# A two-block transformer kernel on one core: packed modulation products, alternating projection blocks, products crossed behind norms and turns in groups

## The chip, the cores and the metric

The kernel runs on one core of a Trainium2 chip. TensorE (PE) multiplies, VectorE (DVE) and ScalarE (ACT) do the element-wise work and empty PSUM, and SyncE (SP) issues the transfers. The metric is the time of one execution on the device in microseconds (us), the median of the runs; less is better.

## The reference

256 tokens of width 1024 go through a first block of two layers (modulated norms, attention, SwiGLU) and a second block of two layers (mLSTM and retention side by side, then a feed-forward part and a gate). Everything is float32.

```python
def first_block(x, c, ctx, c_ctx, ...):                # DEPTH = 2
    for l in range(DEPTH):
        sh_a, sc_a, g_a, sh_f, sc_f, g_f = [m[:, None, :] for m in adaln(c, mod_w[l], mod_b[l])]   # silu(cond) @ mod_w + mod_b
        csh_a, csc_a, cg_a, csh_f, csc_f, cg_f = adaln(c_ctx, mod_w[l], mod_b[l])
        hx = modulate(rms_norm(x, norm_mix_g[l]), sh_a, sc_a)
        hc = modulate(rms_norm(ctx, norm_mix_g[l]), csh_a, csc_a)
        y_x, y_c = even_mixer(...) if l % 2 == 0 else odd_mixer(...)
        x = x + g_a * (y_x @ w_out[l])
        x = x + g_f * swiglu(modulate(rms_norm(x, norm_ffn_g[l]), sh_f, sc_f), ffn_w_in[l], ffn_w_out[l])
        ...                                            # the same for ctx in layer 0
    return x

def second_block(x, p, ...):
    for i in range(DEPTH):
        z = rmsnorm(x, norm1_g[i]) @ w_in[i] + b_in[i]
        _, _, mv, mo, mi, mf, rq, rk, rv, rg, gm, gr = split_cols(z)
        qk = jax.nn.silu(causal_conv(z[..., :2 * M_QK], conv_w[i], conv_b[i]))
        ...
        hm = mlstm_chunkwise(mq, mk, mv, mi, log_sigmoid(mf))
        y_m = sigmoid(mo) * head_layernorm(hm, m_norm_g[i], M_HEADS)
        hr = retention_chunkwise(rope(rq), rope(rk) * R_DK ** -0.5, rv, log_gamma)
        y_r = silu(rg) * head_layernorm(hr, r_norm_g[i], R_HEADS)
        merged = sigmoid(gm) * (y_m @ w_bm[i]) + sigmoid(gr) * (y_r @ w_br[i])
        x = x + merged @ w_out[i]
        x = x + square(relu(rmsnorm(x, norm2_g[i]) @ w_ff1[i] + b_ff1[i])) @ w_ff2[i] + b_ff2[i]
        x = x + sigmoid(rmsnorm(x, norm3_g[i]) @ w_pe_gate[i]) * (p[i] @ w_pe[i])
    return rmsnorm(x, final_g)
```

## The kernel before

**Weights.** All weights come from one array in HBM, cut into 348 chunks of 1 MB: four tiles of 128 rows of the contraction by 512 columns. SP loads them in order into a ring of four slots (`RING`). Most products are made of three: ACT rounds a chunk into `w_hi` (L1085, three slots, `HI_RING`), DVE writes what is left, `w_lo`, in place of the chunk (L1503), the activations are likewise split into `x_hi` and `x_lo`, and `product` (L471 to L476) multiplies hi by hi, lo by hi and hi by lo. 300 chunks go this way; the 48 of the modulation are multiplied as they are. A contraction of 1024 takes two chunks (`kg` 0 and 1) for a block of 512 columns.

**Forms.** `project_feat` gives a block with features on the partitions (256 tokens wide), and its four sub-blocks lie in two banks of PSUM. `project_tok` gives one with tokens on the partitions, 512 wide, in two banks. `project_feat` and `project_tok` alternate between banks 0, 1 and 2, 3 from block to block. `claim(bank)` waits until the bank's last reader is done.

**Order.** The order is written out by hand for each engine. PE's program sets the order of the chunks. ACT and DVE convert chunks at set places of their own programs: `split_for(st, l, j)` (ACT) and `lo_for` (DVE) convert up to `AHEAD` = 2 chunks past the last chunk of a block; `split_to` and `lo_to` go to a given chunk.

**Modulation.** Its 24 blocks of 512 columns are spread over the first block's work. `mod_chunk` (L745) multiplies one raw chunk with the padded condition vectors `cond` (8 matmuls per block at L759), ACT copies the bank to rows (L1240), and `mod_turn` (L731) turns the rows of the block with four small matmuls (L742, two records each in the trace) into columns in bank 4. DVE adds the bias (L1740) and sets `mods_ready` (L1748) for a part of the blocks (`MOD_PARTS`). The first part, blocks 0 to 3, is wanted before the first weight product, that of `ev_in`; squares of X are added for its norm (L584, L587).

**Second block.** Per layer, in PE's order: four blocks mqk (features), the gates, mv and mo (two token blocks each), rqk, then values and scores of the four mLSTM heads (L885, L891) between the blocks rv, those of retention (L903) between gm and gr, turns (`turn`, L599, matmuls at L608) of y_m (`ym`, 8 blocks), w_bm, turns of y_r (`yr`, 16), w_br (8 chunks), turns of merged (`mg`, 8), w_out2 (4 chunks), ff1 and ff2 in halves, pe. For each mqk block DVE scales the result by 1/rms (L1998) into `SCR`, ACT adds the bias and makes the first tap of the convolution (L1410), DVE adds three taps for four channels (12 instructions, L2036) and ACT applies silu. The token blocks get their bias on DVE (L1958, `biased`). `layer_norms` (L1963) norms y_m and y_r on DVE (L1972: subtract the mean, multiply by 1/std, for each head and tile). Behind w_out2 `update` adds to X (L2161), and the tails square X, make `x_hi` (ACT) and `x_lo` (DVE, L1587) as the input of ff1; `after_first` puts the norm's sum of squares after the first chunk of the product behind it.

## Time and profile before

| | |
|---|---|
| median of 3 runs | 2538.41 us |
| lowest, highest | 2537.29, 2539.85 us |
| the profiled execution | 2536.93 us |
| its span on the core | 2535.1 us |
| busy PE / DVE / ACT | 2358.1 / 1520.0 / 1017.4 us |
| mean share of TensorE's full clock | 0.971 |
| moved by DMA | 389.2 MB |

The profile is of one execution. Its views list each engine's instructions with their start, their length and the idle time before them, with what ended that idle time. An idle stretch of an engine that isn't the last to finish costs nothing.

### The profile page before, as it was taken

Reading aid. Unit: us, or ns where it says so; the run is one execution under the profiler, and the core shown is the slowest. Engines: PE = TensorE matmul, PEld = TensorE weight load, DVE = VectorE, ACT = ScalarE, POOL = GpSimd, SP = SyncE. Lnnn points to the kernel's source line nnn. Section 1 sums busy time; section 2 is a strip of 40 time slices with the busy share of each in tenths; the row PEclk is TensorE's granted clock in tenths of the full one; section 3 lists DMA queues with packets and bytes.
Section 4 is the critical chain, followed back from the end, with each engine's and each line's share of the span. In section 5 each row is a group of like instructions: output and inputs, shape, how many; then the busy total and the mean of one; then the engine's idle time right before and its main releaser. Section 6 shows DMA issues by size and latency. Waiting matters only on the chain.

```text
span 2535.1 us, 33331 instructions
## 1 busy us (share of the span) xinstructions
PE 2358.1 (93%) x14334; PEld 2029.4 (80%) x14334; DVE 1520.0 (60%) x1872; ACT 1017.4 (40%) x1222; POOL 0.2 (0%) x4
## 2 busy tenths in 40 slices
PE   5988989999998988999899998999988999999997
PEld 3765667777776757999888876899987978679997
DVE  3787542323246586555666767576666766767575
ACT  4245542221124155334553334444555424344344
POOL 0000000000000000000000000000000000000000
PEclk9989989999998999999999999999999999999998
DMA  6450034444332142555454543455544535344552
GB/s 275 166 199 1 23 138 189 169 163 183 116 106 105 72 100 82 184 183 184 166 195 163 183 170 133 167 177 184 181 153 178 179 145 202 131 161 167 183 183 100
DMA packets 61114, 389.20 MB, mean 154 GB/s; under 512 B 6568, under 2 KB 11048, under 8 KB 15784
## 3 DMA queue, kind: packets, MB, share of 16 engines
q1 hardware_dynamic: 60968, 387.08, 42.2%
q8 instruction: 113, 1.85, 0.3%
q14 instruction: 33, 0.27, 0.0%
HBM read 386.00 MB, written 1.05 MB: 153 GB/s over the span
## 4 chain that ended last, share of the span: by engine, by line
PE 75%; DVE 16%; ACT 5%; issue 3%; DMA 1%; SPq 0%; DVEq 0%; ACTq 0%
PE PS L474 22%; PE PS L475 22%; PE PS L476 22%; DVE w_lo L1503 4%; PE PS L759 2%; DVE BIG L2036 2%; ACT w_hi L1085 1%; PE PS L608 1%; PE PS L903 1%; PE PS L647 1%; PE PS L885 1%; DVE stat L1698 1%; PE PS L742 1%; PE PS L672 1%; DVE SCR L1998 1%
## 5 line engine op out<-in xcount | busy, mean ns | idle before, releaser
L1503 DVE TENSOR_TENSOR w_lo<-raw,w_hi 128x2048 fp32r<-128x2048 f32 x300 | 682.6, 2290 | 564.3 <-ACT w_hi L1085 562.3
L1085 ACT ACTIVATE w_hi<-raw 128x2048 fp32r<-128x2048 f32 x300 | 571.5, 1912 | 761.0 <-PE PS L476 470.0
L474 PE MATMUL PS<-x_hi,w_hi 128*128 128x256 f32 (+1 forms) x2048 | 634.9, 310 | 27.8 <-DVE w_lo L1503 10.9
L475 PE MATMUL PS<-x_lo,w_hi 128*128 128x256 f32 (+1 forms) x2048 | 630.7, 308 | 0.0
L476 PE MATMUL PS<-x_hi,w_lo 128*128 128x256 f32 (+1 forms) x2048 | 630.0, 308 | 0.0
L474 PEld LDWEIGHTS PS<-x_hi,w_hi 128*128 128x128 f32 x2048 | 398.0, 194 | 55.6 <-issue 22.5
L475 PEld LDWEIGHTS PS<-x_lo,w_hi 128*128 128x128 f32 x2048 | 398.0, 194 | 16.4
L476 PEld LDWEIGHTS PS<-x_hi,w_lo 128*128 128x128 f32 x2048 | 397.6, 194 | 16.9
L474 PE MATMUL PS<-w_hi,x_hi 128*128 128x512 f32 (+1 forms) x800 | 319.4, 399 | 29.6 <-DVE w_lo L1503 17.8
L475 PE MATMUL PS<-w_lo,x_hi 128*128 128x512 f32 (+1 forms) x800 | 315.2, 394 | 0.0
L476 PE MATMUL PS<-w_hi,x_lo 128*128 128x512 f32 (+1 forms) x800 | 314.8, 394 | 0.0
L474 PE MATMUL PS<-BIGR,w_hi 128*128 128x256 f32 (+1 forms) x896 | 272.8, 305 | 0.0
L475 PE MATMUL PS<-BIGR,w_hi 128*128 128x256 f32 (+1 forms) x896 | 272.4, 304 | 0.0
L476 PE MATMUL PS<-BIGR,w_lo 128*128 128x256 f32 (+1 forms) x896 | 272.2, 304 | 0.0
L474 PEld LDWEIGHTS PS<-w_hi,x_hi 128*128 128x128 f32 x800 | 153.0, 191 | 72.8 <-DVE w_lo L1503 21.8
L474 PEld LDWEIGHTS PS<-BIGR,w_hi 128*128 128x128 f32 x896 | 171.3, 191 | 10.4 <-issue 1.9
L476 PEld LDWEIGHTS PS<-w_hi,x_lo 128*128 128x128 f32 x800 | 152.9, 191 | 31.9
L475 PEld LDWEIGHTS PS<-w_lo,x_hi 128*128 128x128 f32 x800 | 153.2, 191 | 30.2
L476 PEld LDWEIGHTS PS<-BIGR,w_lo 128*128 128x128 f32 x896 | 171.3, 191 | 7.0
L475 PEld LDWEIGHTS PS<-BIGR,w_hi 128*128 128x128 f32 x896 | 171.3, 191 | 6.7
L475 PE MATMUL PS<-w_lo,BIGR 128*128 128x512 f32 x192 | 76.2, 397 | 0.0
L474 PE MATMUL PS<-w_hi,BIGR 128*128 128x512 f32 x192 | 76.2, 397 | 0.0
(281 smaller groups left out, 2331.9 us busy)
## 6 DMA issues: line engine op xcount, KB each, us to landing
raw<-chunks_in SPq DMA_DIRECT2D x348, 1024.0 KB, 4.8
bias_ring<-brows_in SPq DMA_DIRECT2D x32, 256.0 KB, 5.0
...
```

What stands on the lines that cost most here:

```text
L474: pe.matmul(o, lhs[0], rhs[0], start=start, stop=False, **more)
L475: pe.matmul(o, lhs[0], rhs[1], start=False, stop=False, **more)
L476: return pe.matmul(o, lhs[1], rhs[0], start=False, stop=stop, **more)
L608: mm = pe.transpose(PS[:, bank, t * P:(t + 1) * P], src(b, t), ident)
L647: mm = pe.matmul(PS[:, s + i, 0:d["nk"]], a, b, start=m == 0, stop=m == len(mats) - 1)
L672: mm = pe.matmul(PS[:, b, 0:P], pT_, val, start=j == 0, stop=j == n - 1)
L742: mm = pe.matmul(PS[:, 4, at:at + 2], rows[:, s * P:s * P + P], tab("sel_c"), start=True, stop=True)
L759: mm = pe.matmul(PS[32 * kt:32 * kt + 32, b, :], cond[:, 4 * kg + kt, :], w[:, kt, :], start=kg == 0, stop=kg == 1, skip_group_check=True)
L885: mm = pe.matmul(PS[:, b, cols], qkT[:, 8 + 2 * h + j, s * P:(s + 1) * P], qkT[:, 2 * h + j, s * P:256], start=j == 0, stop=j == 1)
L1085: act.activation(w_hi[:, i % HI_RING, :], ring[:, n % RING, :], ACT.Copy).then_inc(*hi_ready.now(n))
L1503: dve.tensor_tensor(w_lo[:, c % RING, :], ring[:, c % RING, :], w_hi[:, i % HI_RING, :].bitcast(F32), ALU.subtract).then_inc(*lo_ready.now(c))
L2036: ins = dve.scalar_tensor_tensor(o, conv_ins[j % 2][:, s, k:k + 256], wk, o, ALU.mult, ALU.add)
```

## The change

1. **Packs.** `MOD_PACKS` puts the 24 modulation blocks in 7 packs of up to four. The chunks of a pack add into different rows of one bank, since each is multiplied with a shifted slice of `cond`, padded to 38 columns. There is one copy by ACT and one turn (four matmuls) per pack. Two banks serve the packs in place of three.
2. **Alternating.** In the second block mqk blocks (banks 0, 1) alternate with mv 0, mv 1, mo 0, mo 1 (banks 2, 3); the weights and biases are laid out in this order. ACT and DVE convert one or two chunks further ahead there, the gate scan moves behind the second block's taps, silu(j) follows block j, and the sigmoid of mo 0 stands behind silu(3).
3. **Crossed.** The first two blocks behind a norm, of mqk 0 with mv 0, and in w_out2 and ff1 of blocks 0 and 1, take the first chunk of both and then the second of both. The norm's sums stand after two chunks (`after_two`).
4. **Turns in groups.** The ym turns stand before the last values of retention, in banks 4, 5, 0, 1. The yr turns are made eight before w_br, four after its first chunk and four after its second. The mg turns are four after w_br's seventh chunk and four after w_out2's first. The copies on ACT and DVE go with them.
5. **Scores.** DVE multiplies the mLSTM scores with their decay ahead of the bias of rv and the w_lo before it.
6. **Norm of y_r.** The scaling is made by ACT (eight Identity with bias and scale), and the products with gain and gate by DVE in two halves, each of which frees turns.

```diff
-MOD_PARTS = (((0, 1, 2, 3), (4, 5, 10, 11, 6, 7), (8, 9)), (tuple(range(12)),))
+MOD_PARTS = (((0, 1, 2, 3), (4, 5, 6, 7, 10, 11), (8, 9)), (tuple(range(12)),))
+MOD_PACKS = [(0, (0, 1, 2, 3)), (0, (4, 5, 6, 7)), (0, (10, 11)), (0, (8, 9)),
+             (1, (0, 1, 2, 3)), (1, (4, 5, 6, 7)), (1, (8, 9, 10, 11))]
+PACK = 4
+COND_W = 32 + 2 * (PACK - 1)
...
-MOD_BANKS = 3
+MOD_BANKS = 2
...
+                by_row = PS[:, 4, 0:96].rearrange("p (j s c) -> p j s c", s=4, c=2)
+                sel = tab("sel_c")[:, 0:2 * len(js)].rearrange("p (j c) -> p j c", c=2)
                 for s in range(4):
-                    at = 8 * j + 2 * s
-                    mm = pe.matmul(PS[:, 4, at:at + 2], rows[:, s * P:s * P + P], tab("sel_c"), start=True, stop=True)
-                mm.then_inc(*mod_turned.now(l, j))
+                    mm = pe.matmul(by_row[:, js[0]:js[-1] + 1, s, :], rows[:, s * P:s * P + P], sel, start=True, stop=True)
...
-                if kg == 0:
+                first = i == 0 and kg == 0
+                if first:
                     mod_turn()
                     claim(b)
                 c, w = take_raw("mod", l)
+                at = 2 * (PACK - 1 - i)
                 for kt in range(4):
-                    mm = pe.matmul(PS[32 * kt:32 * kt + 32, b, :], cond[:, 4 * kg + kt, :], w[:, kt, :],
-                                   start=kg == 0, stop=kg == 1, skip_group_check=True)
-                mm.then_inc(*projected.now("mod", l, j, kg))
+                    mm = pe.matmul(PS[32 * kt:32 * kt + 32, b, :], cond[:, 4 * kg + kt, at:at + 32], w[:, kt, :],
+                                   start=first, stop=i == last and kg == 1, skip_group_check=True)
+                if i == last and kg == 1:
+                    mm.then_inc(*projected.now("mod", n))
+                    reader[b] = mod_rows.after(n)
+                    state["unturned"] = n
...
-                project_feat("mqk", l, 1, hT[2], freed=evicted("mqk", l), need=copied(("n1", l)), between=after_first(("n1", l)))
...
+                for j in range(4):
+                    if j == 0:
+                        project_feat("mqk", l, 1, hT[2], freed=evicted("mqk", l), side=0, need=copied(("n1", l)), deep=[0])
+                        project_tok("mv", l, 1, KD, lhs, biased=True, side=1, deep=[0])
+                        sum_of_squares(("n1", l), 2, True)
+                    project_feat("mqk", l, 1, hT[2], freed=evicted("mqk", l), n0=j, side=0, need=None if j else copied(("n1", l)),
+                                 deep=None if j else [1])
...
+                    project_tok("mv" if j < 2 else "mo", l, 1, KD, lhs, n0=j % 2, biased=True, side=1,
+                                deep=None if j else [1])
...
+                turn(("ym", l), 8, 2, lambda b, t: hm[t][:, b * P:(b + 1) * P], ready=lambda t: y_ready.after("ym", l))
                 values_pair(l, "r", R_H - 1, rv, 512)
-                turn(("ym", l), 8, 2, lambda b, t: hm[t][:, b * P:(b + 1) * P], ready=lambda t: y_ready.after("ym", l))
...
+                def turn_yr(g):
+                    turn(("yr", l), 4, 2, lambda b, t: hr[t][:, b * P:(b + 1) * P],
+                         ready=lambda t: y_ready.after("yr", l, g // 2), b0=4 * g)
+
+                def turn_mg(g):
+                    turn(("mg", l), 4, 2, lambda b, t: merged[:, t, b * P:(b + 1) * P],
+                         ready=lambda t: stored.after("w_br", l, g, 0), b0=4 * g)
+
+                turn_yr(0)
+                turn_yr(1)
+                project_tok("w_br", l, 2, 16, tokens(yrT), need=copied(("yr", l), 16),
+                            between=at_steps({0: lambda: turn_yr(2), 1: lambda: turn_yr(3), 6: lambda: turn_mg(0)}))
+                project_feat("w_out2", l, 2, hT_b, freed=updated("w_out2", l), need=copied(("mg", l)), crossed=True,
+                             between=at_steps({0: lambda: turn_mg(1)}))
+                need, between = copied(("n2", l)), after_two(("n2", l))
...
+                    project_feat("ff1", l, 4, hT[2], freed=evicted("ff1", l), n0=4 * part, need=need, between=between,
+                                 crossed=part == 0)
...
-                    split_for("mqk", l, j)
+                    after = place_of[plan["last chunk", "mqk", l, j]]
+                    split_to(after + AHEAD + 1)
...
-                    if j:
-                        silu(j - 1)
-                split_for("mv", l, 0)
-                silu(3)
+                    split_to(after + AHEAD + 2)
+                    if j == 0:
+                        act.wait_ge(*gate_abs.after(l))
+                        link(act.activation(gt[:, 2, :], gt[:, 2, :], ACT.Exp, scale=-1.0))
+                        link(act.activation(gt[:, 2, :], gt[:, 2, :], ACT.Ln, bias=small[0:4, 60:61], scale=1.0), gate_act, l)
+                    silu(j)
+                    if j == 3:
+                        in_place("mo", l, 1, mo, ACT.Sigmoid)
...
+                split_for("w_bm", l, 0)
+                act.wait_ge(*shift_ready.after(l))
+                for part in range(2):
+                    for t in range(2):
+                        for h in (2 * part, 2 * part + 1):
+                            i = t * R_H + h
+                            o = hr[t][:, h * 512:(h + 1) * 512]
+                            ins = act.activation(o, o, ACT.Identity, bias=stat[:, 168 + i:169 + i],
+                                                 scale=stat[:, 152 + i:153 + i])
+                    ins.then_inc(*tok_acted.now("hr", l, part))
                 split_for("w_bm", l, 1)
-                copy_turned(("yr", l))
-                split_for("w_br", l, 1)
-                copy_turned(("mg", l))
+                copy_turned(("yr", l), 0, 8)
+                first_br = place_of[plan["first chunk", "w_br", l]]
+                split_to(first_br + 2)
+                copy_turned(("yr", l), 8, 4)
+                split_to(first_br + 3)
+                copy_turned(("yr", l), 12, 4)
+                split_to(first_br + 8)
+                copy_turned(("mg", l), 0, 4)
+                split_to(first_br + 10)
+                copy_turned(("mg", l), 4, 4)
...
+                dve.wait_ge(*tok_acted.after("rg", l, 3, 0))
+                for part in range(2):
+                    cols = slice(1024 * part, 1024 * part + 1024)
+                    dve.wait_ge(*tok_acted.after("hr", l, part))
+                    for t in range(2):
+                        ins = dve.tensor_tensor(hr[t][:, cols], hr[t][:, cols], G[:, 1024:3072][:, cols], ALU.mult)
+                    link(ins)
+                    for t in range(2):
+                        ins = dve.tensor_tensor(hr[t][:, cols], hr[t][:, cols], rg[:, t, cols], ALU.mult)
+                    link(ins, y_ready, "yr", l, part)
+                    lo_to(ahead + 2 + part)
...
+                    conv_scale(j)
+                    lo_to(place_of[plan["last chunk", "mqk", l, j]] + AHEAD + 1)
...
+                    st, dst = ("mv", mv) if j < 2 else ("mo", mo)
+                    if j == 1:
+                        lo_for(st, l, 1)
+                        dve.wait_ge(*gate_act.after(l))
...
                     arg(h)
-                    biased("rv", l, 1, wide(rv), h)
                     dve.wait_ge(*exp_ready.after("m", l, h))
                     link(dve.scalar_tensor_tensor(SCR[:, 384 * (h % 2):384 * (h % 2) + 384], PS[:, 4, 0:384],
                                                   QK_SCALE, SCR[:, 768 + 384 * (h % 2):1152 + 384 * (h % 2)],
                                                   ALU.mult, ALU.mult), probs_ready, "m", l, h)
+                    biased("rv", l, 1, wide(rv), h)
...
+                copy_turned(("ym", l))
                 r_out(R_H - 1)
-                copy_turned(("ym", l))
-                layer_norms(l, "hr", hr, 512, G[:, 1024:3072], rg)
+                norm_r(l)
```

**Order, PE, start of the program.** L759 and L783 are the modulation's chunks, L742 and L762 the turns, L584 and L592 the norm's sums, L474 and L479 the first weight products. Before:

```order
L759 MATMUL PS<-raw,bias_ring 32x512 x8
L742 MATMUL PS<-tabt,SCR 128x2 x4
L759 MATMUL PS<-raw,bias_ring 32x512 x8
L584 MATMUL PS<-tabt,G 128x1 x4
L587 MATMUL PS<-G,tabt 128x512
L742 MATMUL PS<-tabt,SCR 128x2 x4
L759 MATMUL PS<-raw,bias_ring 32x512 x8
L742 MATMUL PS<-tabt,SCR 128x2 x4
L759 MATMUL PS<-raw,bias_ring 32x512 x8
L742 MATMUL PS<-tabt,SCR 128x2 x4
L474 MATMUL PS<-w_hi,x_hi 128x448
```

The changed kernel:

```order
L783 MATMUL PS<-raw,bias_ring 32x512 x16
L592 MATMUL PS<-tabt,G 128x1 x4
L595 MATMUL PS<-G,tabt 128x512
L783 MATMUL PS<-raw,bias_ring 32x512 x16
L762 MATMUL PS<-tabt,SCR 128x4x2 x4
L479 MATMUL PS<-w_hi,x_hi 128x448
```

The four turns became one, behind all eight chunks; the sums stand between the fourth and the fifth chunk.

**Order, DVE, mqk stage of layer 0.** L1503 and L1559 make w_lo, L1998 and L2075 scale, L2036 and L2104 are the taps, L1958 and L2015 the bias of a token block. Before:

```order
L2036 SCALAR_TENSOR_TENSOR BIG<-BIG,colt 128x256 x12
L1503 TENSOR_TENSOR w_lo<-raw,w_hi 128x2048 x2
L1998 TENSOR_TENSOR SCR<-PS,G 128x1024
L2036 SCALAR_TENSOR_TENSOR BIG<-BIG,colt 128x256 x12
L1503 TENSOR_TENSOR w_lo<-raw,w_hi 128x2048 x2
```

The changed kernel:

```order
L2104 SCALAR_TENSOR_TENSOR BIG<-BIG,colt 128x256 x12
L2015 SCALAR_TENSOR_TENSOR free_a<-PS,stat,bias_ring 128x512 x2
L1559 TENSOR_TENSOR w_lo<-raw,w_hi 128x2048 x2
L2075 TENSOR_TENSOR SCR<-PS,G 128x1024
L1559 TENSOR_TENSOR w_lo<-raw,w_hi 128x2048
L2104 SCALAR_TENSOR_TENSOR BIG<-BIG,colt 128x256 x12
L1559 TENSOR_TENSOR w_lo<-raw,w_hi 128x2048
```

Per mqk block there are now four w_lo in place of two, one of them between the scale and the taps, and a token block's bias.

**Order, DVE, first head of the mLSTM, layer 0.** L2103 and L2183 multiply the scores with the decay. Before:

```order
L2096 SCALAR_TENSOR_TENSOR SCR<-PS,small,tabt 128x128
L1503 TENSOR_TENSOR w_lo<-raw,w_hi 128x2048 [waits hi_ready,exp_arg]
L1503 TENSOR_TENSOR w_lo<-raw,w_hi 128x2048 [waits hi_ready]
L1958 SCALAR_TENSOR_TENSOR BIG<-PS,stat,bias_ring 128x512 [waits bias_in1,projected]
L1958 SCALAR_TENSOR_TENSOR BIG<-PS,stat,bias_ring 128x512
L2103 SCALAR_TENSOR_TENSOR SCR<-PS,SCR 128x384 [waits exp_ready]
```

The changed kernel:

```order
L2177 SCALAR_TENSOR_TENSOR SCR<-PS,small,tabt 128x128
L2183 SCALAR_TENSOR_TENSOR SCR<-PS,SCR 128x384 [waits exp_ready,exp_arg]
L1559 TENSOR_TENSOR w_lo<-raw,w_hi 128x2048 [waits hi_ready,probs_ready]
L1559 TENSOR_TENSOR w_lo<-raw,w_hi 128x2048 [waits hi_ready]
L2015 SCALAR_TENSOR_TENSOR BIG<-PS,stat,bias_ring 128x512 [waits bias_in0,projected]
L2015 SCALAR_TENSOR_TENSOR BIG<-PS,stat,bias_ring 128x512
```

The product moved ahead of two w_lo and the bias of rv.

**Order, PE, last values of retention and the ym turns.** L903 and L929 are the values, L608 and L626 the turns. Before:

```order
L903 MATMUL PS<-BIG,SCR 128x512 [waits y_out,probs_ready]
L903 MATMUL PS<-BIG,SCR 128x512 x2
L903 MATMUL PS<-BIG,SCR 128x512 [waits y_out,probs_ready]
L903 MATMUL PS<-BIG,SCR 128x512 x2
L608 MATMUL PS<-tabt,xn 128x128 [waits y_ready,probs_ready]
L608 MATMUL PS<-tabt,xn 128x128 [waits y_ready]
L608 MATMUL PS<-tabt,xn 128x128 [waits probs_ready]
L608 MATMUL PS<-tabt,xn 128x128
L608 MATMUL PS<-tabt,xn 128x128 [waits y_out]
```

The changed kernel:

```order
L929 MATMUL PS<-BIG,SCR 128x512 [waits y_out,probs_ready]
L929 MATMUL PS<-BIG,SCR 128x512 x2
L626 MATMUL PS<-tabt,xn 128x128 [waits y_ready,probs_ready]
L626 MATMUL PS<-tabt,xn 128x128 [waits y_ready]
...
L626 MATMUL PS<-tabt,xn 128x128 [waits stored]
L626 MATMUL PS<-tabt,xn 128x128
L626 MATMUL PS<-tabt,xn 128x128 [waits copied_v]
L626 MATMUL PS<-tabt,xn 128x128
...
L626 MATMUL PS<-tabt,xn 128x128
L929 MATMUL PS<-BIG,SCR 128x512 [waits y_out,probs_ready]
L929 MATMUL PS<-BIG,SCR 128x512 x2
L479 MATMUL PS<-w_hi,BIGR 128x512 [waits copied_v,lo_ready]
```

The turns moved ahead of the last values, from the third block on they wait for readers of their banks, and only the values stand before w_bm (L479).

## Rows read from the trace of the kernel before

**Rows 1.** The page: busy time, share of the span and instructions of each engine.
```profile
PE 2358.1 (93%) x14334; PEld 2029.4 (80%) x14334; DVE 1520.0 (60%) x1872; ACT 1017.4 (40%) x1222; POOL 0.2 (0%) x4
```

**Rows 2.** PE's waits, whole run: engine, line, waited for, total us, times, longest.
```profile
PE PS L474 <- DVE w_lo L1503: 28.7, 12, 6.3
...
PE PS L608 <- DVE bias_ring L1740: 7.0, 1, 7.0
...
PE PS L885 <- DVE SCR L2103: 7.3, 2, 3.7
```

**Rows 3.** PE's timeline, modulation turns: start us, us, instruction, idle before it.
```profile
85.77 0.95 PE L742 MATMUL PS<-tabt,SCR 128*128 128x2 f32 x8
86.65 0.64 PE L759 MATMUL PS<-raw,bias_ring 128*32 128x512 f32 x4
...
655.74 1.87 PE L742 MATMUL PS<-tabt,BIG 128*128 128x2 f32 x8 [5.48 <-ACT BIG L1240]
```

**Rows 4.** Stretches: length, busy PE, PEld, DVE, ACT, POOL, PEclk, DMA share, GB/s.
```profile
1198.00:1310.00 112.00, 103.80 (x640) 93.32 (x641) 75.73 (x102) 61.44 (x71) 0.00 (x0) 0.94 0.46 169
1858.20:1970.20 112.00, 101.08 (x627) 90.87 (x628) 74.86 (x101) 61.42 (x71) 0.00 (x0) 0.95 0.45 164
1372.20:1375.50 3.30, 3.27 (x9) 2.69 (x10) 0.00 (x0) 0.00 (x0) 0.00 (x0) 0.51 0.14 60
2034.90:2044.50 9.60, 9.56 (x23) 7.17 (x24) 2.92 (x3) 2.32 (x2) 0.00 (x0) 0.50 0.06 24
1520.20:1563.80 43.60, 36.92 (x157) 27.59 (x156) 39.26 (x55) 17.97 (x30) 0.00 (x0) 0.92 0.33 121
1197.90:1201.50 3.60, 3.56 (x17) 3.59 (x18) 3.60 (x11) 3.01 (x7) 0.00 (x0) 0.53 0.21 82
```

**Rows 5.** PE's timeline at the start of the program.
```profile
20.58 1.86 PE L742 MATMUL PS<-tabt,SCR 128*128 128x2 f32 x8 [9.37 <-ACT SCR L1240]
22.38 3.64 PE L759 MATMUL PS<-raw,bias_ring 128*32 128x512 f32 x16
...
43.35 1.87 PE L742 MATMUL PS<-tabt,SCR 128*128 128x2 f32 x8 [0.72 <-ACT SCR L1240]
51.53 0.74 PE L474 MATMUL PS<-w_hi,x_hi 128*128 128x448 f32 x1 [6.31 <-DVE w_lo L1503]
```

**Rows 6.** ACT's timeline at the start, squares of X.
```profile
14.22 1.67 ACT L1114 ACTIVATE G<-X 128x512 f32<-128x512 f32 x3 [10.77 <-DMA X<-ctx_in]
```

**Rows 7.** DMA over the first 50 us, in 40 slices.
```profile
GB/s 0 112 324 419 377 430 426 426 433 439 419 433 426 419 419 419 419 419 262 0 85 433 426 413 321 0 0 0 39 341 419 334 406 190 295 433 465 393 452 385
```

**Rows 8.** PE's waits in the mqk stage of layer 0, then of layer 1.
```profile
PE PS L474 <- DVE w_lo L1503: 8.1, 3, 3.9
...
PE PS L474 <- DVE w_lo L1503: 10.9, 4, 3.9
```

**Rows 9.** DVE's timeline in the mqk stage, layer 0.
```profile
1240.14 5.10 DVE L2036 SCALAR_TENSOR_TENSOR BIG<-BIG,colt 128x256 f32<-128x256 f32 x12 [3.88 <-ACT BIG L1410]
1245.15 4.49 DVE L1503 TENSOR_TENSOR w_lo<-raw,w_hi 128x2048 fp32r<-128x2048 f32 x2
```

**Rows 10.** ACT's timeline, a table load and what follows.
```profile
1207.46 1.28 ACT L1138 ACT_TABLE_LOAD   x1
1208.76 0.26 ACT L1138 ACTIVATE stat<-PS,small 128x2 f32<-128x2 f32 x1
```

**Rows 11.** DVE's timeline before the first mLSTM values, layer 0.
```profile
1371.62 0.55 DVE L2103 SCALAR_TENSOR_TENSOR SCR<-PS,SCR 128x384 f32<-128x384 f32 x1
```

**Rows 12.** DVE's timeline, scaling of hr, layer 0.
```profile
1534.81 1.92 DVE L1972 TENSOR_SCALAR free_a<-free_a,stat 128x512 f32<-128x512 f32 x4
```

**Rows 13.** PE's timeline, turns of merged, layer 0.
```profile
1610.29 3.38 PE L608 MATMUL PS<-tabt,SCR 128*128 128x128 f32 x16 [2.67 <-DVE SCR L2141]
```

**Rows 14.** PE's timeline, first product of ff1, layer 0.
```profile
1637.43 0.39 PE L474 MATMUL PS<-x_hi,w_hi 128*128 128x256 f32 x1 [0.36 <-DVE x_lo L1587]
```

**Rows 15.** ACT's timeline, last w_hi inside w_out2, layer 0.
```profile
1631.41 1.92 ACT L1085 ACTIVATE w_hi<-raw 128x2048 fp32r<-128x2048 f32 x1 [1.75 <-PE PS L476]
```

371 lines of the change are left out of this document (197 added, 174 removed).

## The prediction

> **What bounds the kernel now.** I read the page's busy shares first, then the waits of PE, then the stretches around each wait. PE is busy 93% of the span, mostly at the full clock (2.4 GHz) [rows 1]: a change that removes no weight product can win at most the 7% of idle time, the small PE work beside the products, and the stretches at the lower clock (1.2 GHz). The idle time is not one wait. Its largest item is PE waiting for DVE's w_lo, 28.7 us in 12 waits; the waits for the scores of the mLSTM are 7.3 in two [rows 2]. So I go through the program by place and ask at each which wait ends last. Durations are of the profiled execution, 2536.93 us (span 2535.1), which is 1.5 under the median of the runs, 2538.41.
>
> A wait costs twice: after it the rows show PE at the lower clock. The same turn of eight records takes 0.95 us at one level and 1.87 at the other [rows 3], and the stretches behind the waits show a granted clock of 0.50 to 0.53 [rows 4]. I charge half of such a stretch as lost.
>
> **Start, packing.** Before, the turn of modulation block 0 waits 9.37 us for ACT's copy of the block, and ACT has that copy behind its squares of X, for which ctx landed only at 14.22 [rows 5, 6]. Blocks 0 to 3 have four turns, of 1.86 or so each, and the last two wait 0.72 each for the copy [rows 5]. The change puts the four blocks in one pack: one copy, one turn. Chunks 2 and 3 then need no turn ahead; the DMA gives about 0.42 MB per us while it is busy [rows 7], so they land 2.5 and 5 us after ctx, at 16.7 and 19.2, and are multiplied by 21.1 (1.82 a chunk: 3.64 for two [rows 5]), against 26.0 before. That is −4.9. Behind the norm's sums and root, which keep their length, two chunks, a wait, a turn, two chunks, a wait and a turn shrink to four chunks, a wait and one turn: −(2 × 1.8 + 0.72) = −4.3, of which I take 4.1. Together **−9.0** (bounds −7 and −11: the DVE work that turns rows into factors stays and its wait of 6.31 before the first product stays too).
>
> **Packing, later.** A turn at full clock holds PE 0.88 us, from 85.77 to the next instruction's start at 86.65 [rows 3]. Of 24 turns 7 stay. Of the other 17, three belong to the start, and two save nothing: at 655.74 PE waits for a copy that stands behind a w_hi, which waits for its chunk's DMA, so a turn less ahead of it only lengthens the wait [rows 3], and one at 176 is followed by the 7.0 us wait for the factors of L1740, whose end is set by a transfer [rows 2]. Twelve are left: 12 × 0.88 = **−10.6** (−7 to −12). The chunks' own matmuls are the same number; ACT loses 17 copies, which were covered.
>
> **Alternating blocks (mqk with mv and mo).** Before, DVE does per mqk block: 12 taps 5.10, two w_lo 4.49, a scale (L1998, 1.2) and a wait of 3.88 for ACT's first taps, together 14.7 us [rows 9]. PE needs less for the block's two chunks: the 103.8 us of PE in the stretch from 1198 to 1310 [rows 4] hold 17 chunks, the gates' products (3.4) and some 5 lost to the clock, so 5.6 a chunk and 11.2 a block. PE catches up with DVE and has then waited 8.1 us in layer 0 and 10.9 in layer 1 [rows 8]. The clock: the mean of 0.94 over 112 us is 6.7 us lost, of which the first stretch, behind the norm, is 1.7 and stays, so 5.0; the mean of 0.95 in layer 1 gives 5.6, less as much for its own first stretch, 3.9 [rows 4]. After, between two mqk blocks stands a token block, so one round is four chunks, 22.4 of PE. DVE has 1.2 + 5.1 + four w_lo 9.0 + 1.4 for the bias = 16.7, and 1.9 more in the round with the gate scan, 18.6. DVE now has slack in every round, and the wait for ACT's taps lies beside w_lo work that was put there (the second pair of order pieces above). I followed all rounds on the three engines and found no stall, with 1 to 4 us to spare. So all of it goes: 8.1 + 10.9 + 5.0 + 3.9 = **−27.9**. Bounds: nothing saved in half of the rounds (−14), and no more than −28, since the products stay.
>
> The change also adds one ACT table load per layer here (sigmoid of mo before and after an exp). A load takes 1.28 us, and the activation starts 0.02 behind it [rows 10]; ACT is busy 61.4 of 112 us in this stretch [rows 4], so 1.3 is hidden and the sum has no term for it. The Trainium skill, "ScalarE: Activation LUTs", section What ACT_TABLE_LOAD costs, speaks against more switches: beside the load it gives about 1.38 us of drain for each, 2.66 in all. By that the sum would be up to 3 us worse over both layers, where the slack of 1 us is gone at the place of the load. The trace shows no such drain, since ACT's instructions around the load stand back to back.
>
> **Scores of the mLSTM.** PE's L885 waits twice, 7.3 us in all [rows 2], for DVE's L2103, the product of the scores with the decay. It is short, 0.55 [rows 11], but stood behind two w_lo and the bias of rv. The change puts it ahead of them. Two waits 7.3, the stretches at the lower clock behind them 3.3 and 9.6 us [rows 4], half lost, 6.4: **−13.7** (−7 if the w_lo, now later, are what PE waits for instead; w_lo has two chunks of lead there).
>
> **The m and r outputs.** From the end of gr's last product to the start of w_br's turns and product DVE is busy 39.26 of 43.6 us [rows 4]: DVE bounds this place, not PE. The change takes eight scalings of 0.48 off DVE [rows 12] (3.8 us) and gives them to ACT, but DVE must now wait for ACT, and ACT has two w_hi before them. PE's wait ahead of yr's turns goes, since turns are cut in groups of four, but PE waits 3 us at the ym turns (they stand before the last r values, and their banks 0, 1 come free only from DVE) and some 5 before the fifth yr turn. By hand w_br starts 1.6 to 3.3 us earlier, but 1.7 us of turns now stand inside w_br, and a new stretch at the lower clock takes 1.7 or less. Sum **+0.5** per layer, **+1.0** (−6 to +6).
>
> **mg turns into w_out2.** Before, a wait of 2.67 and 16 turns at the lower clock, 3.38 [rows 13]. After, eight turns stand before the last w_br chunk and eight behind the first w_out2 chunk, at full clock 1.7 for all. 2.67 + 1.7, and 0.3 of the first products at the lower clock: −4.7 a layer, **−9.4**. If PE waits at the second group it is −5.
>
> **Crossing w_out2 and ff1.** Both blocks of w_out2 now end one chunk apart instead of two. The tail of a block is: ACT's squares and x_hi, DVE's add, x_lo, squares. Before, its last x_lo came 0.36 us late [rows 14]. After, ACT's w_hi (1.92) and behind it DVE's w_lo (2.25) [rows 9, 15] of the chunk that ff1 needs first stand between the two tails: w_hi starts 3.2 before the end of w_out2, w_lo 1.3 before it, the add 1.0 after it, and the last x_lo 2.9 after it. So +2.5, and 0.9 for the clock, per layer: **+6.8** (0 to +9). What crossing is meant to give at the other norms I take as nothing: those waits end with the first input, not with the second half.
>
> **Sum.** −9.0 − 10.6 − 27.9 − 13.7 + 1.0 − 9.4 + 6.8 = −62.8. 2536.9 − 62.8 = 2474.1 for the profiled run, and with the 1.5 between it and the median 2476.
>
> **Rivals.**
> 1. The alternating stage still starves PE. If DVE is late by 1.5 us in every round (it was up to 3.9 late before), and half of a stretch like the one of 3.3 us [rows 4] is lost behind each, 8 rounds cost 8 × 3.15 = 25: 2501. For it: slack of 1 us at two w_lo, and a third w_lo ahead of the taps. Against it: 22.4 against 18.6.
> 2. The mg groups give only 5 of 9.4 (+4.4) and y costs +2.5 a layer more (+5): 2485.
> 3. The tail of w_out2 isn't late, and the yr path gains the 3 us a layer: 2466.
> 4. Slower: the look-ahead breaks in the alternating stage. If each of its 32 chunks is converted only when PE has freed the slot, w_hi 1.92 and w_lo 2.25 stand open, 4.2 × 32 = 134 less 63: 2610. It decides from 15 chunks on. Against it: ring and slots are as before, and the order puts w_lo two or three chunks ahead.
> 5. The packing doesn't shorten the start (copy still behind squares) and of all the rest only the scores move: 2538.4 − 13.7 = 2525.
>
> **How the numbers follow.** Forecast (2470 to 2482) 0.55; rival 1 0.14; rival 2 0.12; rival 3 0.12; rival 4 0.02; rival 5 0.03; the rest lies between them. The range takes in the forecast, rivals 1 to 3: 2460 to 2502. A measurement of this kernel tells 0.2% (5 us) from no change. Only rival 4 is slower, and "the same" needs 58 of 63 us to fail: faster 0.95, same 0.02, slower 0.03.
>
> **What would show it.** The first L479 at about 42.5 (before 51.53). No wait for w_lo in the mqk stage, and a clock of 0.98 or more in it. No wait for the scores. Seven turns L762. PE busy about 2343 of a span of 2473. A wait of about 3 us at the first ff1 product. I am wrong if PE waits for w_lo at every second chunk of the stage, or if mg's second group of turns waits for DVE.

## The result and the profile after

| | before | changed |
|---|---|---|
| median of the runs | 2537.9 us (4 runs, 2537.29 to 2539.85) | 2473.17 us (4 runs, 2470.73 to 2477.3) |
| profiled execution, its span | 2536.93, 2535.1 | 2472.95, 2471.2 |
| ratio | | 0.9745, 95% interval 0.9728 to 0.9762 |

The change makes the kernel 2.55% faster, 64.7 us; 2476 was forecast. The page of the changed kernel, busy time and the granted clock in slices (to set beside [rows 1]):

```profile
PE 2316.3 (94%) x14198; PEld 1993.9 (81%) x14198; DVE 1514.4 (61%) x1866; ACT 1019.5 (41%) x1223; POOL 0.2 (0%) x4
...
PEclk9999999999998999999999999999999999999999
```

PE is busy 42 us less, and idle 22 us less; part of the 42 is the lower clock (the mean share of the full clock rose from 0.971 to 0.976), since the weight products are the same. In the changed kernel PE's waits over the whole run (what is waited for, total us, times, longest) are, against [rows 2]:

```profile
PE PS L626 <- DVE BIGR L1580: 16.1, 4, 5.2
PE PS L479 <- DVE w_lo L1559: 14.8, 8, 7.5
...
PE PS L479 <- DVE x_lo L1643: 9.7, 3, 4.7
```

The waits for w_lo fell from 28.7 to 14.8 us, those for the scores are gone, and waits for turned blocks (`BIGR`, the copies of the y_m and y_r turns, 8.4 us before) have doubled to 16.1: that is what the change built.

To see where 64 us went, I cut both traces at the same places of the program: the first weight product, the first mqk product of each layer (1197.94 and 1858.10 before, 1176.21 and 1818.02 after), the first scores, the end of gr's last product (1520.18 and 1479.24 in layer 0), the end of w_br and of w_out2. The group of mg turns that now stands inside w_br, some 0.9 us, is counted with the mg turns. The differences of the lengths:

| part | forecast | measured |
|---|---|---|
| start to first weight product | −9.0 | −10.7 |
| from there to the second block (turns) | −10.6 | −11.0 |
| mqk, mv, mo stage and rqk, both layers | −27.9 | −29.1 (−13.3, −15.8) |
| scores of the mLSTM | −13.7 | −14.9 (−5.9, −8.9) |
| y_m, y_r, w_bm, w_br | +1.0 | +4.1 (+2.1, +2.1) |
| mg turns, w_out2 | −9.4 | −9.2 |
| ff1 start and the rest | +6.8 | +6.9 |
| sum | −62.8 | −63.9 |

The sum is that of the two profiled spans, 2471.2 − 2535.1.

**Start.** PE's timeline of the changed kernel, to set beside [rows 5] (start us, us, instruction, idle before it):

```profile
16.99 1.94 PE L783 MATMUL PS<-raw,bias_ring 128*32 128x512 f32 x8 [5.61 <-DMA raw<-chunks_in]
...
26.51 4.97 PE L783 MATMUL PS<-raw,bias_ring 128*32 128x512 f32 x32
32.20 1.06 PE L762 MATMUL PS<-tabt,SCR 128*128 128x8 f32 x8 [0.73 <-ACT SCR L1285]
40.79 0.74 PE L479 MATMUL PS<-w_hi,x_hi 128*128 128x448 f32 x1 [7.53 <-DVE w_lo L1559]
```

Chunk 2 comes at 16.99, as its transfer lands, one turn stands behind the eighth chunk, and the first weight product is at 40.79 in place of 51.53. The single turn took 1.06 us and four chunks 4.97, not 1.87 and 7.3: the granted clock had risen during the last four chunks, which the sum had left at the lower level. These are 3.1 us, of which a longer wait for w_lo, 7.53 in place of 6.31, takes 1.2 back, which leaves 1.9 and so about the 1.7 us beyond the forecast.

**Stage of the alternating blocks.** Windows of both layers in the changed kernel (length, then busy PE, PEld, DVE, ACT, POOL, granted clock, DMA share, GB/s), against the first two of [rows 4]:

```profile
1180.00:1320.00 140.00, 140.00 (x998) 130.77 (x997) 106.30 (x122) 80.92 (x87) 0.00 (x0) 1.00 0.54 194
1822.00:1962.00 140.00, 140.00 (x998) 130.76 (x997) 106.72 (x123) 81.31 (x87) 0.00 (x0) 1.00 0.54 194
```

PE is busy in all of the 140 us, at the full clock: no wait is left to win here. DVE's timeline of one round, to set beside [rows 9]:

```profile
1218.83 1.22 DVE L2075 TENSOR_TENSOR SCR<-PS,G 128x1024 f32<-128x1024 f32 x1
1220.23 2.29 DVE L1559 TENSOR_TENSOR w_lo<-raw,w_hi 128x2048 fp32r<-128x2048 f32 x1 [0.19 <-ACT w_hi L1131]
1223.95 5.09 DVE L2104 SCALAR_TENSOR_TENSOR BIG<-BIG,colt 128x256 f32<-128x256 f32 x12 [1.43 <-ACT BIG L1445]
1228.96 2.28 DVE L1559 TENSOR_TENSOR w_lo<-raw,w_hi 128x2048 fp32r<-128x2048 f32 x1
```

The wait for ACT's taps is 1.43 us in place of 3.88, since a w_lo (at 1220.23) lies in it.

**Scores.** DVE's timeline at the first head, to set beside [rows 11]:

```profile
1329.09 0.56 DVE L2183 SCALAR_TENSOR_TENSOR SCR<-PS,SCR 128x384 f32<-128x384 f32 x1 [0.67 <-ACT SCR L1479]
1330.89 4.49 DVE L1559 TENSOR_TENSOR w_lo<-raw,w_hi 128x2048 fp32r<-128x2048 f32 x2 [1.24 <-ACT w_hi L1131]
1335.30 1.40 DVE L2015 SCALAR_TENSOR_TENSOR BIG<-PS,stat,bias_ring 128x512 f32<-128x512 f32 x2
```

The product with the decay (L2183) stands ahead of the two w_lo, which it had been behind.

**Turns of y_r.** PE's timeline, then DVE's:

```profile
1520.76 0.42 PE L626 MATMUL PS<-tabt,free_a 128*128 128x128 f32 x1 [5.18 <-DVE BIGR L1580]
```

```profile
1513.61 2.29 DVE L1559 TENSOR_TENSOR w_lo<-raw,w_hi 128x2048 fp32r<-128x2048 f32 x1
1515.82 1.22 DVE L2214 TENSOR_TENSOR SCR<-PS,X 128x1024 f32<-128x1024 f32 x1
1516.95 2.28 DVE L1559 TENSOR_TENSOR w_lo<-raw,w_hi 128x2048 fp32r<-128x2048 f32 x1
1519.15 1.22 DVE L2214 TENSOR_TENSOR SCR<-PS,X 128x1024 f32<-128x1024 f32 x1
1520.29 1.41 DVE L1580 TENSOR_TENSOR BIGR<-PS,BIGR 128x256 fp32r<-128x256 f32 x4
```

PE waits 5.18 us before the fifth block of y_r. Its bank is one of four and still holds the first block, whose copy (L1580, from 1520.29) stands on DVE behind two w_lo and both evictions of w_bm (L2214).

**mg turns.** PE's timeline, to set beside [rows 13]:

```profile
1563.23 1.03 PE L626 MATMUL PS<-tabt,SCR 128*128 128x128 f32 x8
...
1575.31 1.04 PE L626 MATMUL PS<-tabt,SCR 128*128 128x128 f32 x8
```

Neither group waits, and both run at the full clock. No run undoes these groups alone: their 9.2 us are read from the lengths and these rows.

**ff1.** The first product behind w_out2 waits 2.46 us, where 2.9 were forecast and 0.36 stood before [rows 14]:

```profile
1596.07 0.58 PE L479 MATMUL PS<-x_hi,w_hi 128*128 128x256 f32 x1 [2.46 <-DVE x_lo L1643]
```

### The profile page after: what moved, and what is told of

Read it like the earlier page. It is cut to its first block, busy times and chain, and to the rows that moved or that the text cites. A ratio compares the mean times of both kernels' runs of the same rounds, so it can differ in the third digit from the quotient of the medians.

```text
span 2471.2 us, 33032 instructions
## 1 busy us (share of the span) xinstructions
PE 2316.3 (94%) x14198; PEld 1993.9 (81%) x14198; DVE 1514.4 (61%) x1866; ACT 1019.5 (41%) x1223; POOL 0.2 (0%) x4
## 4 chain that ended last, share of the span: by engine, by line
PE 83%; DVE 9%; ACT 3%; issue 3%; DMA 2%; SPq 0%; DVEq 0%; ACTq 0%
PE PS L479 25%; PE PS L480 25%; PE PS L481 25%; DMA raw<-chunks_in 1%; PE PS L929 1%; ACT w_hi L1131 1%; PE PS L783 1%; DVE w_lo L1559 1%; PE PS L626 1%; PE PS L665 1%; DVE stat L1754 1%; PE PS L911 1%; PE PS L690 1%; ACT xn L1209 1%; DVE BIG L1763 1%
## 5 line engine op out<-in xcount | busy, mean ns | idle before, releaser
L1559 DVE TENSOR_TENSOR w_lo<-raw,w_hi 128x2048 fp32r<-128x2048 f32 x300 | 684.3, 2290 | 537.3 <-ACT w_hi L1131 535.4
L479 PE MATMUL PS<-x_hi,w_hi 128*128 128x256 f32 (+1 forms) x2048 | 631.9, 309 | 22.7 <-DVE x_lo L1643 9.7
L479 PEld LDWEIGHTS PS<-x_hi,w_hi 128*128 128x128 f32 x2048 | 396.2, 193 | 49.3 <-issue 22.1
L479 PE MATMUL PS<-w_hi,x_hi 128*128 128x512 f32 (+1 forms) x800 | 317.3, 397 | 22.6 <-DVE w_lo L1559 10.6
L479 PE MATMUL PS<-BIGR,w_hi 128*128 128x256 f32 (+1 forms) x896 | 272.8, 304 | 0.0
L479 PEld LDWEIGHTS PS<-w_hi,x_hi 128*128 128x128 f32 x800 | 152.0, 190 | 63.8 <-issue 19.8
L479 PEld LDWEIGHTS PS<-BIGR,w_hi 128*128 128x128 f32 x896 | 171.3, 191 | 10.4 <-issue 3.6
L479 PE MATMUL PS<-w_hi,BIGR 128*128 128x512 f32 x192 | 77.6, 404 | 2.4 <-DVE w_lo L1559 2.4
```

The lines of the kernel that those rows point to most:

```text
L479: pe.matmul(o, lhs[0], rhs[0], start=start, stop=False, **more)
L1559: dve.tensor_tensor(w_lo[:, c % RING, :], ring[:, c % RING, :], w_hi[:, i % HI_RING, :].bitcast(F32), ALU.subtract).then_inc(*lo_ready.now(c))
```

## Experiments

Each kernel ran once, with a profile; the last two ran four times. The runs were made on three chips, and the kernel before ran beside them: 2541.81 us beside the first four experiments, 2538.64 beside the next four, 2538.73 (median of 7, 2535.67 to 2540.59) beside the last four. The same kernel differs by some us from run to run, and much of that arises in the first block, which no experiment but singles touches: the second block of these kernels began at 1175.5 to 1180.6 us. So I compare the lengths of the two layers of the second block, from first mqk product to first mqk product, and from the second one to the end of the span:

| kernel | median or single time | layer 0 | layer 1 and end | both against the changed kernel |
|---|---|---|---|---|
| before | 2537.9 | 660.2 | 677.1 | +42.3 |
| changed | 2473.2 | 641.8 | 653.2 | 0 |
| seq_plain | 2498.3 | 653.0 | 666.6 | +24.6 |
| seq_ahead | 2481.9 | 645.0 | 656.6 | +6.6 |
| scores_late | 2485.2 | 646.2 | 660.1 | +11.3 |
| singles | 2501.5 | 641.0 | 653.1 | −0.8 |
| finish_first | 2469.3 | 637.5 | 649.4 | −8.1 |
| uncross_out | 2468.5 | 639.6 | 650.0 | −5.4 |
| y_dve | 2472.7 | 639.4 | 652.9 | −2.7 |
| y_fine | 2471.0 | 640.8 | 652.8 | −1.3 |
| ym_split | 2468.8 | 640.2 | 650.4 | −4.4 |
| yr_cross | 2461.4 | 634.8 | 646.3 | −13.8 |
| best | 2449.0 (4 runs) | 629.6 | 640.5 | −24.9 |
| after_again | 2477.5 (4 runs) | 641.4 | 654.1 | +0.5 |

Two rows of the last column tell how far the same work repeats: the second block of singles (−0.8) and of after_again (+0.5) is that of the changed kernel. I read no number below 3 us as a gain.

### The alternation undone, and undone with its look-ahead kept

seq_plain, PE's program (ACT, DVE and the weights' order as in the kernel before):

```diff
-                for j in range(4):
-                    ...                      # mqk j, then mv or mo
+                project_feat("mqk", l, 1, hT[2], freed=evicted("mqk", l), need=copied(("n1", l)), between=between)
+                ...
+                project_feat("mqk", l, 3, hT[2], freed=evicted("mqk", l), n0=1)
+                ...
+                project_tok("mv", l, 2, KD, lhs, biased=True)
+                project_tok("mo", l, 2, KD, lhs, biased=True)
```

> The changed kernel with the alternation alone undone: four mqk blocks, then mv and mo, and ACT and DVE in the order of the kernel before in this stage (the first products of mqk and mv are then not crossed either). If my sum is right, DVE is short in this stage again: PE waits 8 us in layer 0 and 11 in layer 1 for w_lo and loses 4 to 5 us more to the lower clock in each, so 2473 + 28 = 2501. If the stage's gain came from something else that the change did (the packs, the earlier start), nothing comes back here: 2473 to 2476.

> Four mqk blocks in a row as before, but ACT and DVE keep the look-ahead of the changed kernel: one w_lo stands between the scale and the taps, while DVE would wait for ACT's taps. Theory 1 (alternation is what gives DVE its slack): DVE needs 10.8 us of work per mqk block of 11.2 to 11.5 us of PE, with nothing to spare for any wait, so some of the stalls stay: 2473 + 10 to 15 = 2483 to 2488. Theory 2 (the wait of 3.9 us for the taps was the whole fault, and the look-ahead fills it): PE waits less than 2 us for w_lo per layer and the time is 2473 to 2477, so alternating is not needed.

seq_ahead has the same program on PE, but DVE and ACT keep most of the changed kernel's order. These lines of DVE's program stay:

```diff
                     conv_scale(j)
                     lo_to(place_of[plan["last chunk", "mqk", l, j]] + AHEAD + 1)
```

So do three more differences to seq_plain: ACT converts its w_hi one or two chunks further ahead; silu(j) follows block j; and the gates' Exp and Ln (ACT) stand behind its first tap of block 0 and their scan (DVE) behind the taps of block 1, where seq_plain has both ahead of the taps of block 0.

PE's waits in layer 0 of this stage, of seq_plain and then of seq_ahead (what is waited for, total, times, longest):

```profile
PE PS L479 <- DVE w_lo L1555: 9.4, 4, 3.9
```

```profile
PE PS L479 <- DVE w_lo L1555: 2.7, 3, 1.3
```

DVE's waits in the same stretch, of seq_plain and then of seq_ahead (the taps' line is L2108 in one and L2099 in the other), and PE's first wait in seq_plain:

```profile
DVE BIG L2108 <- ACT BIG L1445: 12.1, 4, 3.9
...
DVE rowt L2094 <- ACT rowt L1426: 2.4, 1, 2.4
```

```profile
DVE BIG L2099 <- ACT BIG L1443: 4.8, 3, 1.7
```

```profile
1211.91 0.58 PE L479 MATMUL PS<-x_hi,w_hi 128*128 128x256 f32 x1 [3.94 <-DVE w_lo L1555]
```

seq_plain gives back 24.6 us (time +25), nearly what was forecast: the stage is where that gain lay. seq_ahead gives back only 6.6, and its waits for w_lo are 2.7 where seq_plain has 9.4. So **three quarters of the stage's gain, 18 of 24.6 us, come from the new order on DVE and ACT, and one quarter from the order on PE** (the alternation with its crossed first products), which I had argued was the cause.

Two things in that order can be seen in the rows, and no run parts them. A w_lo now lies in DVE's wait for the taps: one mqk block takes DVE 14.52 us in seq_plain (its taps start at 1233.60 and 1248.12) and 12.32 in seq_ahead (1233.01 and 1245.33). And the gates no longer stand ahead of the first taps: in seq_plain DVE waits 2.37 us for ACT there and then makes the scan and the taps, and the w_lo behind these is what PE waits 3.94 us for, the longest of its waits. In layer 1 the picture is the same, with 8.3 and 2.7 us of waits.

Neither theory's number was met: seq_ahead gives back less than the 10 to 15 us of the first, and its 2.7 us of waits in each layer are more than the "less than 2" of the second. The 12.32 us of a block on DVE are still more than the 11.5 of PE (from 1206.50 to 1218.02 in the changed kernel), and in the changed kernel, where token blocks lie between, no wait is left.

### The scores

```diff
                     arg(h)
+                    biased("rv", l, 1, wide(rv), h)
                     dve.wait_ge(*exp_ready.after("m", l, h))
                     ...
-                    biased("rv", l, 1, wide(rv), h)
```

> The changed kernel with one move undone: DVE's product of the mLSTM scores with the decay stands behind the bias of rv again. If its place was the cause, PE waits 3.7 us in each layer before its second scores and loses 1.6 to 4.8 us after each to the lower clock: +10 to +14, 2483 to 2487. If the wait was a sign of DVE being late from the mqk stage, it does not come back: 2473.

PE's waits of scores_late around the first scores of layer 0, then the place in layer 1 in its timeline:

```profile
PE PS L911 <- DVE SCR L2184: 3.7, 1, 3.7
```

```profile
1984.31 1.22 PE L911 MATMUL PS<-BIG 128*128 128x256 f32 x2 [3.65 <-DVE SCR L2184]
```

The wait is back with its 3.65 us in each layer, though DVE was not late from the mqk stage. Its place in DVE's program was the cause. The layers are 4.4 and 6.9 us longer, and the time, 2485.2, lies in the range expected.

### The packs

```diff
-MOD_PACKS = [(0, (0, 1, 2, 3)), (0, (4, 5, 6, 7)), (0, (10, 11)), (0, (8, 9)),
-             (1, (0, 1, 2, 3)), (1, (4, 5, 6, 7)), (1, (8, 9, 10, 11))]
+MOD_PACKS = [(l, (j,)) for l, j in MOD_SEQ]
-MOD_BANKS = 2
+MOD_BANKS = 3
```

with 24 copies in ACT's program, at the places of the kernel before.

> The changed kernel with the packs undone: 24 copies by ACT and 24 turns, one for each block of the modulation, with the blocks in the changed order. By my sum 9 us at the start and 12 turns of 0.88 us come back: first weight product at 51.5 in place of 40.8, and the time 2473 + 20 to 22 = 2493 to 2495. A rival says that the turns were hidden in waits elsewhere, and only the start comes back: 2484.

PE's timeline of singles at the start:

```profile
20.63 1.86 PE L761 MATMUL PS<-tabt,SCR 128*128 128x2 f32 x8 [9.36 <-ACT SCR L1284]
...
43.40 1.87 PE L761 MATMUL PS<-tabt,SCR 128*128 128x2 f32 x8 [0.72 <-ACT SCR L1284]
51.58 0.74 PE L478 MATMUL PS<-w_hi,x_hi 128*128 128x448 f32 x1 [6.32 <-DVE w_lo L1566]
```

The start is that of the kernel before (51.58, [rows 5]), and the second block starts at 1205.59, 29.4 us after that of the changed kernel. I had expected 20 to 22. Of the 29.4 the start gives back 10.8 (51.58 for 40.79) and the later turns 18.6, where the change had gained 11.0. With its own 4.3 us more at the lower clock (half lost: 2) and with the 1 to 4 us by which the other runs of the changed first block began later than the first one (1177.6 in the mean), I estimate that some 24 to 26 remain. The kernel before, with the same 24 turns, took 1197.94, 7.6 less than singles: its PE is busy 5.0 us less ahead of the second block (1090.4 for 1095.4) and waits 2.6 less. What makes this isn't settled. The order of blocks 6, 7, 10 and 11 differs, and two waits of the first block are 1.2 and 0.9 us longer in singles (2.60 for 1.40, 2.98 for 2.04); but the kernel before, run beside singles, took 2541.81 us too, 3.9 above its first median, and its profile wasn't kept. So the turns are worth 11 us by one comparison and up to 15 by the other.

### w_out2 and ff1

finish_first, in DVE's `update`:

```diff
+                            if i == 0 and j and st == "w_out2":
+                                finish(key, before)
+                                before = []
                             if i == 0:
                                 lo_for(st, l, j)
```

> The changed kernel, and DVE finishes the last two tiles of w_out2's block 0 (x_lo and the squares) before it makes the w_lo for ff1 and waits for block 1. My theory of the wait of 2.46 us before ff1 is that these two tiles stand behind a w_lo and the add of block 1. Then the wait goes in both layers, and the stretch of 3.4 us at the lower clock with it: -2.46 - 1.7 each, 2473 - 8 = 2465. If the wait is ACT's (its squares and x_hi stand behind a w_hi), the first product of ff1 waits as before: 2473.

uncross_out:

```diff
-                project_feat("w_out2", l, 2, hT_b, freed=updated("w_out2", l), need=copied(("mg", l)), crossed=True,
+                project_feat("w_out2", l, 2, hT_b, freed=updated("w_out2", l), need=copied(("mg", l)),
```

> The changed kernel with w_out2 uncrossed alone: block 0 takes both chunks, then block 1. By the prediction crossing costs 3.4 us a layer at ff1, so -6.8; but the second group of mg turns is now followed at once by the chunk that needs it, and PE waits 1 to 1.5 us for the copies, +2.5 and some clock: 2473 - 3 = 2470 (2466 to 2473). If crossing covers more than it costs, it is 2475 or more, with a wait of over 2.5 us behind the second mg group.

DVE's timeline of finish_first, and PE's of uncross_out:

```profile
1594.60 0.48 DVE L1643 SCALAR_TENSOR_TENSOR x_lo<-X,colt,x_hi 128x256 fp32r<-128x256 f32 x1
...
1596.24 2.29 DVE L1559 TENSOR_TENSOR w_lo<-raw,w_hi 128x2048 fp32r<-128x2048 f32 x1 [0.82 <-ACT w_hi L1131]
```

```profile
1578.26 0.39 PE L479 MATMUL PS<-x_hi,w_hi 128*128 128x256 f32 x1 [1.27 <-DVE x_lo L1580]
...
1596.15 0.39 PE L479 MATMUL PS<-x_hi,w_hi 128*128 128x256 f32 x1 [0.36 <-DVE x_lo L1643]
```

In finish_first the x_lo of block 0 (L1643, last at 1594.60) are ready before the w_lo at 1596.24, PE waits for nothing before ff1, and the layers are 8.1 us shorter, as expected. So the wait was DVE's order, and not ACT's. uncross_out has the old wait of 0.36 and a new one of 1.27 behind the second mg group, and its layers are 5.4 us shorter. Without the 1.27 (2.5 over both layers) it would be 7.9 by estimate, where 6.8 had been forecast for the crossing. finish_first gets as much with w_out2 still crossed, by DVE's order alone.

### The way to y_r

y_dve takes the scaling back to DVE. y_fine cuts the y_r turns finer; here are its lines on PE, and on DVE the eviction of w_bm's first block and the copies of the first four turns move ahead of the second half of y_r:

```diff
-                turn_yr(1)
                 ...
-                            between=at_steps({0: lambda: turn_yr(2), 1: lambda: turn_yr(3), 6: lambda: turn_mg(0)}))
+                            between=at_steps({0: lambda: turn_yr(1), 1: lambda: turn_yr(2), 2: lambda: turn_yr(3),
+                                              6: lambda: turn_mg(0)}))
```

> The changed kernel with the scaling of y_r back on DVE (8 x 0.48 us in each layer). If DVE bounds the place from the last values of retention to w_br, w_br starts 3.8 us later less the waits for ACT that go (2.4 us of DVE's waiting behind its second w_lo): +1.5 to +3.8 a layer, 2476 to 2481. If ACT is the bound there, it is the same or faster: 2470 to 2473.

> The changed kernel with the y_r turns cut finer: four before w_br and four behind each of its first three chunks; DVE makes the first half of y_r, empties w_bm's first block and copies the first four turns before it makes the second half. The wait of 5.18 us in each layer before the fifth turn is now a wait of 1.5 to 2 for the first copies, and w_br starts 5 to 6 us earlier; the later turns wait for nothing. -4 to -6 a layer: 2461 to 2465. If DVE's total work bounds the place wherever it stands, the same time returns as waits for w_lo or copies inside w_br: 2473.

PE's timeline of y_fine in w_br (rows that waited):

```profile
1515.53 0.50 PE L479 MATMUL PS<-w_hi,BIGR 128*128 128x512 f32 x1 [1.27 <-DVE BIGR L1583]
...
1523.84 0.50 PE L479 MATMUL PS<-w_hi,BIGR 128*128 128x512 f32 x1 [1.69 <-DVE BIGR L1583]
...
1539.69 0.50 PE L479 MATMUL PS<-w_hi,BIGR 128*128 128x512 f32 x1 [1.27 <-DVE BIGR L1583]
```

y_dve is no slower (2472.7), against the 1.5 to 3.8 us a layer expected: the 3.8 us that ACT takes off DVE are lost in waits for ACT (1.54 us before a w_lo at 1497.12 and 2.41 before the products with the gain at 1501.83; y_dve has neither). That part of the change brings nothing. y_fine missed its 4 to 6 us a layer: it removes the 5.18 us and puts four waits of 1.27 to 1.69 in their place, each before the chunk that follows its group of turns at once. It is not DVE's total work, as yr_cross shows.

ym_split cuts the y_m turns around the last values of retention:

```diff
-                turn(("ym", l), 8, 2, ...)
+                turn(("ym", l), 4, 2, ...)
                 values_pair(l, "r", R_H - 1, rv, 512)
+                turn(("ym", l), 4, 2, ..., b0=4)
```

> The changed kernel with the y_m turns cut in two: blocks 0 to 3 before the last values of retention, 4 to 7 behind them, in banks 4, 5, 2, 3, so that no turn waits for a copy of the four before it. The wait of 2.86 us in each layer goes, w_bm starts 2 to 3 us earlier, and DVE's chain to y_r with it: -3 to -4 a layer, 2465 to 2467. If DVE's chain starts no earlier, PE waits as much longer before the y_r turns: 2473.

yr_cross crosses the two blocks of w_br for half of the contraction, so that one chunk lies between a group of turns and its use. Beside these lines on PE, DVE evicts both blocks of w_bm and copies the first four turns ahead of the last products with the gate:

```diff
-                turn_yr(1)
-                project_tok("w_br", l, 2, 16, tokens(yrT), need=copied(("yr", l), 16), ...)
+                steps = at_steps({0: lambda: turn_yr(1), 2: lambda: turn_yr(2), 3: lambda: turn_yr(3), 6: lambda: turn_mg(0)})
+                for j, deep in ((0, [0]), (1, [0]), (0, [1]), (1, [1]), (0, [2, 3]), (1, [2, 3])):
+                    project_tok("w_br", l, 1, 16, tokens(yrT), need=copied(("yr", l), 16), n0=j, deep=deep, between=steps)
```

> The changed kernel with w_br's two blocks crossed for the first half of the contraction (block 0 and 1 with the first chunk each, then with the second each), the second group of y_r turns behind the first chunk, and one chunk of 5.4 us between each group of turns and its use, which the finer cut lacked: its waits of 1.3 us behind each group should be gone, and the wait of 5.2 us before the fifth turn becomes one of 1.5 to 2 for the first copies. -5 to -7 a layer: 2459 to 2463. If DVE's work is what is short, waits for w_lo or for copies of 4 us or more appear in w_br: 2470 or more.

yr_cross is 13.8 us shorter, with one wait of 1.27 left before the first chunk of w_br, where the turns still are followed at once by their use; the three later waits of y_fine are gone. The orders on DVE differ too, so the runs don't show what each of the two moves gives. ym_split is 4.4 shorter, where 6 to 8 were expected: the wait of 2.86 goes, but one of 0.60 comes before the last values, and the wait for w_lo inside w_bm grows from 1.20 to 1.85.

### The three together, and the changed kernel once more

> The three edits together: y_m turns in two halves, w_br crossed with the y_r turns one chunk ahead, and the two tiles of w_out2's block 0 finished first. If they are as independent as their places, the gains add: 4 (half of 8) + 12 + 7 less what the lower clock gives back, 2473 - 23 = 2450 (2445 to 2458). If DVE's chain is the bound through the whole of y_m and y_r, one of the first two gives nothing beside the other: 2460.

> The changed kernel itself once more, on the chip of the runs beside it, so that they can be set against it: 2470 to 2477, as in its first four runs. The rows of the first profile should come back to 0.1 us at each wait, and what differs between runs should be the stretches at the lower clock.

PE's timeline of best, rows around the y_m and y_r turns:

```profile
1483.19 1.04 PE L626 MATMUL PS<-tabt,xn 128*128 128x128 f32 x8
1484.83 2.81 PE L929 MATMUL PS<-BIG,SCR 128*128 128x512 f32 x6 [0.60 <-DVE free_b L2184]
1487.48 1.04 PE L626 MATMUL PS<-tabt,xn 128*128 128x128 f32 x8
...
1506.74 0.50 PE L479 MATMUL PS<-w_hi,BIGR 128*128 128x512 f32 x1 [1.89 <-DVE w_lo L1563]
...
1514.62 0.50 PE L479 MATMUL PS<-w_hi,BIGR 128*128 128x512 f32 x1 [1.27 <-DVE BIGR L1584]
```

best, with finish_first, ym_split and yr_cross, runs in 2448.97 us (2448.39 to 2451.47, 4 runs), 0.9651 of the kernel before (0.9635 to 0.9667); on the same chip the changed kernel took 2477.45 (2474.56 to 2480.68), which is 0.9761 (0.9746 to 0.9775). The layers are 24.9 us shorter, where 8.1 + 4.4 + 13.8 = 26.3 would be the sum of the parts: the gains are nearly independent. The wait for w_lo inside w_bm grew from 1.20 to 1.89 us. after_again stands at the upper edge of the 2470 to 2477 expected, and two of its four runs lie above.

## Why the prediction was right

The time lay 3 us under the forecast, and most steps held one by one, as the table of parts shows. That the profiled run came within 1.2 us of the sum (2472.95 for 2474.1) is partly luck: the parts miss by 8 us when their signs are left out. In detail:

- **Start**: the mechanism was right and the gain 1.7 us too small, since the clock had risen for the last four chunks and the turn.
- **Turns**: 11.0 for 10.6. In the experiment that undid them they cost more, and some 4 us of it stay unexplained.
- **Alternating stage**: the size was right, 29.1 for 27.9 (24.6 when undone alone), but the reason was only partly so. "DVE now has slack in every round" named the alternation; three quarters come from the order on DVE and ACT. Both were in the sum, so it could not tell them apart. Two counts in it were wrong and nearly cancelled: the stretch from 1198 to 1310 holds 16 chunks, not 17, and the gates' products take 5.5 us (1211.91 to 1217.36), not 3.4. A chunk of mqk takes 5.8 us and one of mv or mo 5.45, and the round of four comes to the 22.4 of the forecast (1206.50 to 1228.92).
- **Scores**: right in wait, place and clock (14.9 for 13.7). When undone alone it gave back 11.3, with 4 us for the clock in place of 6.4.
- **y_m and y_r**: +4.1 where +1.0 stood. The waits had the forecast sizes (2.86 for "3 us", 5.18 for "some 5"); the term that was mis-sized is w_br's start, 1.6 to 3.3 us earlier by hand, and 0.55 by the trace (1563.82 to 1522.33, of 40.94 by which everything ahead had moved). The scaling on ACT, counted as 3.8 us off DVE, brought nothing: the waits for ACT, which the prediction named but did not price, took it back.
- **mg and crossing**: 9.2 for 9.4, 6.9 for 6.8. The mechanism at ff1, tiles of block 0 behind a w_lo and the add of block 1, was shown by finish_first. For mg no run undoes the groups.
- **Table loads**: PE was busy in all of both windows of 140 us, so the added loads cost nothing. The drain that the prediction cited from the Trainium skill, "ScalarE: Activation LUTs", What ACT_TABLE_LOAD costs, shows in no row here: at the added load ACT's instruction ahead ends at 1274.95 and the load starts at 1274.97.
- **Signs**: the first product at 40.79 (42.5 was given), no wait in the stage, none for the scores, seven turns and 2.46 us at ff1 came as said. PE's busy time did not: 2316.3 us, where 2343 was given. That figure didn't follow from the sum's own terms: its waits, 19.0 for w_lo, 7.3 for the scores and 5.3 at mg less 5.0 at ff1, are some 27 us, and the other 36 are busy time.
- **Rivals**: none of them came in whole; rival 1's waits were zero, not 1.5. Of rival 2, y did cost 1.6 us a layer more (2.5 there), but the mg groups gave all of their 9.2. Rival 3's terms, 6.8 and 3 a layer off the forecast's sum, would come to 2462 or 2463, not 2466.
